# Prompt attention of a decoder step: scores over two pairs of PSUM banks, the last projection tiles by token halves, the conv mixer in pieces, block outputs copied to SBUF

## The reference

```python
gb, gc, u, q, k, v = split(rmsnorm(x) @ w_in)          # 3 x 512 conv mixer, 3 x 512 attention
yconv = gb * causal_dwconv(gc * u, prefix, w3, b)      # width 3, over tokens
s  = einsum('bqhcd,bkhcd->bhcqk', q, k) / 8 + bias     # 4 heads, c = 2 halves of 64; causal, T5 bias
p  = softmax(s)
o  = (p[c=0] - lam * p[c=1]) @ v
yattn = rmsnorm(o) * w * (1 - lam_init)                # per head of 128
x += concat(yconv, yattn) @ w_out
x += cross_attn(rmsnorm(x), memory K/V)
x += conv_ffn(rmsnorm(x))
y  = rmsnorm(x)
```

## Time and profile before

| | |
|---|---|
| time, median of 3 runs | 1035.6 us (1034.36 to 1038.36) |
| the profiled execution | 1035.47 us, span 1033.0 us |
| TensorE busy | 967.5 us (94%) |
| weight loads of TensorE | 884.1 us (86%) |
| VectorE busy | 560.5 us (54%) |
| ScalarE busy | 361.8 us (35%) |
| GpSimd busy | 97.9 us (9%) |
| granted clock of TensorE, mean | 0.98 of full speed |

### The profile page before, as it was taken

One profiled execution on the slowest core, in us unless ns is written; L12 is line 12 of the kernel. 1 busy time (PEld: TensorE's weight loads), 2 busy tenths in 40 slices (PEclk: granted clock), 3 DMA queues, 4 the chain that ended last, 5 costly groups with the idle time before them and its releaser, 6 DMA issues.

```text
span 1033.0 us, 19196 instructions
## 1 busy us (share of the span) xinstructions
PE 967.5 (94%) x7675; PEld 884.1 (86%) x7675; DVE 560.5 (54%) x1021; ACT 361.8 (35%) x670; POOL 97.9 (9%) x213
## 2 busy tenths in 40 slices
PE   5999999978988999999889999999999999999996
PEld 4977766747878999988656999999999999999995
DVE  4544523626677645335433448777347783477643
ACT  4422212223445436234323334343124331234332
POOL 2220000000000012000000002221012220122000
PEclk8999998998999999999999999999999999999998
DMA  8656678841111246624652422233233232323213
GB/s 236 206 175 212 202 240 284 276 158 42 42 41 42 84 123 196 214 81 155 233 205 101 97 82 83 82 98 88 82 91 94 82 88 85 94 85 95 72 37 103
DMA packets 162491, 131.36 MB, mean 127 GB/s; under 512 B 5819, under 2 KB 139222, under 8 KB 162370
## 3 DMA queue, kind: packets, MB, share of 16 engines
q1 hardware_dynamic: 159940, 124.40, 39.0%
q0 software_dynamic: 2320, 5.68, 1.9%
q10 hardware_dynamic: 144, 0.07, 0.0%
HBM read 123.12 MB, written 7.00 MB: 126 GB/s over the span
## 4 chain that ended last, share of the span: by engine, by line
PE 81%; DVE 7%; issue 4%; ACT 3%; SPq 2%; DMA 2%; DVEq 0%; ACTq 0%
PE proj L942 66%; PE T L954 7%; PE score L1031 2%; PE score L1147 1%; PE score L1132 1%; PE score L1059 1%; SPq L665 1%; DVE score L1790 1%; ACT pages L1392 1%; DMA w_raw<-in_w_in 1%; SPq L682 1%; PE score L1165 1%; ACT w_hi L1227 1%; DVE a_lo L1593 1%; DVE norm_area L1587 0%
## 5 line engine op out<-in xcount | busy, mean ns | idle before, releaser
L942 PE MATMUL proj<-a_hi,w_hi 128*128 128x272 f32 (+1 forms) x992 | 222.7, 296 | 4.2 <-DVE a_lo L1593 2.6
L942 PE MATMUL proj<-a_hi,w_lo 128*128 128x272 f32 (+1 forms) x992 | 216.5, 289 | 0.0
L942 PE MATMUL proj<-a_lo,w_hi 128*128 128x272 f32 (+1 forms) x992 | 216.4, 289 | 0.0
L1527 DVE TENSOR_TENSOR w_lo<-w_raw,w_hi 128x1024 fp32r<-128x1024 f32 (+1 forms) x132 | 159.0, 1205 | 62.5 <-ACT w_hi L1227 62.2
L1227 ACT ACTIVATE w_hi<-w_raw 128x1024 fp32r<-128x1024 f32 (+1 forms) x132 | 137.2, 1039 | 159.3 <-PE proj L942 143.0
L942 PEld LDWEIGHTS proj<-a_hi,w_hi 128*128 128x128 f32 x992 | 162.0, 191 | 15.2 <-issue 12.5
L942 PEld LDWEIGHTS proj<-a_lo,w_hi 128*128 128x128 f32 x992 | 162.4, 191 | 0.1
L942 PEld LDWEIGHTS proj<-a_hi,w_lo 128*128 128x128 f32 x992 | 160.9, 191 | 0.0
L942 PE MATMUL proj<-d_hi,w_hi 128*128 128x272 f32 x704 | 145.4, 288 | 0.0
L942 PE MATMUL proj<-d_hi,w_lo 128*128 128x272 f32 x704 | 144.8, 288 | 0.0
L942 PE MATMUL proj<-d_lo,w_hi 128*128 128x272 f32 x704 | 144.6, 287 | 0.0
(11 more groups left out here) (257 smaller groups left out, 1219.3 us busy)
## 6 DMA issues: line engine op xcount, KB each, us to landing
w_raw<-in_w_up SPq DMA_DIRECT2D x44, 512.0 KB, 3.8
w_raw<-in_w_in SPq DMA_DIRECT2D x24, 512.0 KB, 5.0
pages<-in_cache_k SPq DMA_DIRECT2D x40, 256.0 KB, 4.4
early_pages<-in_cache_v SPq DMA_DIRECT2D x40, 256.0 KB, 4.5
w_raw<-in_w_ckv SPq DMA_DIRECT2D x16, 512.0 KB, 3.9
c_pages<-in_cache_mem_k SPq DMA_DIRECT2D x16, 512.0 KB, 6.6
c_pages<-in_cache_mem_v SPq DMA_DIRECT2D x16, 512.0 KB, 5.2
w_raw<-in_w_down SPq DMA_DIRECT2D x16, 448.0 KB, 3.7
```

Of the source, the lines that this page charges most:

```text
L942: mm = pe.matmul(proj[n % 2][:, half, 0:width], wt, act[:, k, half * HALF:half * HALF + width], start=(k == 0 and a == 0), stop=(k == w["k ...
L1527: dve.tensor_tensor(w_lo[:, n % W_RING, 0:kt, :], w_raw[:, n % W_RING, 0:kt, :], w_hi[:, n % W_HI_RING, 0:kt, :].bitcast(F32), ALU.subtrac ...
```

## The change

- The tiles of a channel come as gc, u, gb instead of gb, gc, u.
- The tile before the ticks is gone. The last 8 tiles of w_in (channel 1's u to channel 3's gb) are cut by token halves: half 0 has 24 matmuls over all k for tokens 0 to 271, half 1 the same for the others. Tick u, 0 to 15, has one of them. Both go to `proj[0]`, one bank each, and VectorE empties each bank by itself. A half waits until the same bank's last half is emptied.
- `proj[1]` is free for a second pair of score banks, S2 and S3. Odd units use it. A score waits for the exponentials of two units before.
- ScalarE copies a block's outputs from T1 to `o_blk` and frees T1; the squares are taken from `o_blk`, and `p_scale` works in place there.
- The conv mixer of a channel is four steps (rstd and states; first tap; two taps; gating) placed one by one in ticks 3 to 16, with its own buffer `mixed`.

```diff
-        for j, kind in enumerate(("gb", "gc", "u")):
+        for j, kind in ((1, "gc"), (2, "u"), (0, "gb")):
...
+FIRST_BY_HALF, AFTER_IN = TILE["in", "u", 1], TILE["out", "add", 0]
+BY_HALF = range(FIRST_BY_HALF, AFTER_IN)
...
-        if f[1] == "u":
-            part = part + [("conv", f[2]), ("mix", f[2])]
+        if f == ("in", "gb", 0):
+            part = part + [("conv", 0, part) for part in range(3)] + [("mix", 0)]
...
+    beside = {3: [("conv", 1, 0)], 4: [("conv", 1, 1)], 5: [("conv", 1, 2)], 7: [("mix", 1)],
+              9: [("conv", 2, 0)], 10: [("conv", 2, 1)], 11: [("conv", 2, 2)], 13: [("mix", 2)],
+              14: [("conv", 3, 0)], 15: [("conv", 3, 1), ("conv", 3, 2)], 16: [("mix", 3)]}
+    for u in range(len(units) + 2):
+        if 0 <= u - 1 < len(units):
+            s.append(("p_mix", *units[u - 1]))
+        if u >= 4 and units[u - 4][1] == HEADS - 1:
+            s.append(("p_out", units[u - 4][0]))
+        if u < len(units):
+            s.append(("p_score", *units[u]))
+        if 3 <= u < len(units) + 3 and units[u - 3][1] == HEADS - 1:
+            s.append(("p_scale", units[u - 3][0]))
+        if u == 0:
+            s.append(("s_out", 1))
+        n, half = divmod(u, 2)
+        if n < len(BY_HALF):
+            if half == 0:
+                s.append(("split", FIRST_BY_HALF + n + 2))
+            s += beside.get(u, [])
+            s.append(("half", FIRST_BY_HALF + n, half))
+            if half:
+                s.append(("tile", FIRST_BY_HALF + n))
+        else:
+            s += beside.get(u, [])
+        if 0 <= u - 1 < len(units):
+            s.append(("p_turn", *units[u - 1]))
+        if u == len(units) + 1:
+            s.append(("mem_in",))
+        if 0 <= u - 2 < len(units):
+            s.append(("p_pv", *units[u - 2]))
+            if units[u - 2][1] == HEADS - 1:
+                s += [("p_norm", units[u - 2][0]), ("p_eps", units[u - 2][0])]
+    s += [("p_scale", 3), ("half_tile", AFTER_IN), ("p_out", 3)]
+    s += [("squares", k, "mem") for k in range(KT)]
...
+        if kind == "p_score":
+            uses = [use(slot) for slot in (("S0", "S1"), ("S2", "S3"))[(step[1] * HEADS + step[2]) % 2]]
...
+            def tile_half(n, half):
+                if half == 0:
+                    pe.wait_ge(w_lo_ready, n + 1)
+                    if n == FIRST_BY_HALF:
+                        wait_tile_out(pe, n - 2)
+                if n > FIRST_BY_HALF:
+                    pe.wait_ge(half_out, 2 * (n - 1 - FIRST_BY_HALF) + half + 1)
+                cols = slice(half * HALF, (half + 1) * HALF)
+                out = proj[0][:, half, 0:HALF]
+                for k in range(KT):
+                    w_h, w_l = w_hi[:, n % W_HI_RING, k, :], w_lo[:, n % W_RING, k, :]
+                    pe.matmul(out, w_h, a_hi[:, k, cols], start=(k == 0), stop=False)
+                    pe.matmul(out, w_h, a_lo[:, k, cols], start=False, stop=False)
+                    mm = pe.matmul(out, w_l, a_hi[:, k, cols], start=False, stop=(k == KT - 1))
+                mm.then_inc(tile_done if half else half_done, 1)
...
                 elif kind == "p_out":
-                    wait_taken(pe, *use_of["p_norm", arg][0])
+                    pe.wait_ge(sem("p_scaled"), arg + 1)
...
                 elif kind == "p_norm":
                     wait_full(act, uses[0])
+                    if arg:
+                        act.wait_ge(full["T0"], use_of["p_out", arg - 1][0][1] + 1)
+                    act.activation(o_blk, bank["T1"], ACT.Copy).then_inc(free["T1"], 1)
+                    wait_taken(act, *uses[0])
                     for h in range(HEADS):
                         cols = slice(h * P, (h + 1) * P)
-                        ins = act.activation(o_sq[:, cols], bank["T1"][:, cols], ACT.Square,
+                        ins = act.activation(o_sq[:, cols], o_blk[:, cols], ACT.Square,
...
+                elif kind == "half":
+                    w, half = TILES[arg], step[2]
+                    dve.wait_ge(tile_done if half else half_done, arg + 1 if half else arg - FIRST_BY_HALF + 1)
+                    cols = slice(half * HALF, (half + 1) * HALF)
+                    out = proj[0][:, half, 0:HALF]
+                    if w["kind"] == "u":
...
+                        side(dve.tensor_tensor(pre[:, 2 + half * HALF_P:2 + (half + 1) * HALF_P], out[:, mine],
+                                               gate[:, mine], ALU.mult))
+                        dve.tensor_tensor(pre_s[:, GB * half:GB * half + GB, 2:6],
...
+                    else:
+                        dst = gates[:, int(w["kind"] == "gb"), cols]
+                        if w["kind"] == "gb":
+                            dve.wait_ge(sem("mixer_ready"), w["i"])
+                        dve.tensor_tensor(dst, out, rstd[:, cols], ALU.mult).then_inc(half_out, 1)
...
                 elif kind == "p_scale":
                     dve.wait_ge(sem("p_rstd"), arg + 1)
-                    wait_full(dve, uses[0])
-                    dve.tensor_tensor(o_blk.rearrange("p (h d) -> p h d", h=HEADS), quads["T1"],
-                                      free_dims(small[:, 32:36], 0, [(1, HEADS), (0, DV)]), ALU.mult
-                                      ).then_inc(free["T1"], 1)
+                    o = o_blk.rearrange("p (h d) -> p h d", h=HEADS)
+                    dve.tensor_tensor(o, o, free_dims(small[:, 32:36], 0, [(1, HEADS), (0, DV)]), ALU.mult
+                                      ).then_inc(sem("p_scaled"), 1)
```

More of the change, by code:

```diff
@@ L155, in make_schedule @@
     fill = [("in", "k", h) for h in range(HEADS)] + [("in", "v", h) for h in range(HEADS)]
-    fill += [("in", kind, c) for c in range(CT) for kind in ("gb", "gc", "u")]
+    fill += [("in", kind, c) for c in range(CT) for kind in ("gc", "u", "gb")]
     after = {("in", "k", h): [("k_out", h)] for h in range(HEADS)}
@@ L186, in make_schedule @@
     units = [(i, h) for i in range(SEQ // P) for h in range(HEADS)]
[L188 to L211, removed]
+    assert len(plan) == FIRST_BY_HALF - TILE["in", "k", 0]
     late = []
@@ L919, in tile @@
                 pe.wait_ge(w_lo_ready, n + 1)
-                if n >= 2:
+                if n == AFTER_IN:
+                    wait_tile_out(pe, n - 1)
+                elif n == AFTER_IN + 1:
+                    for slot in ("S2", "S3"):
+                        wait_taken(pe, slot, latest[slot])
+                elif n >= 2:
                     wait_tile_out(pe, n - 2)
@@ L994, in _ @@
                               start=True, stop=True).then_inc(full["S0"], 1)
+                elif kind == "half":
+                    tile_half(*step[1:])
                 elif kind in ("tile", "half_tile"):
-                    tile(arg, latest, kind == "half_tile")
+                    if arg not in BY_HALF:
+                        tile(arg, latest, kind == "half_tile")
                 elif kind in ("k_out", "v_out"):
@@ L1077, in _ @@
                             wait_tile_out(pe, TILE["in", "k", hh])
+                    if (i, h) == (0, 1):
+                        wait_tile_out(pe, FIRST_BY_HALF - 1)
                     for half in range(i // 2 + 1):
@@ L1683, in _ @@
                 elif kind == "conv":
+                    c, part = step[1:]
                     settle()
-                    wait_tile_out(dve, TILE["in", "u", arg])
-                    side(dve.tensor_tensor(by_half(pre[:, 2:2 + SEQ]), by_half(pre[:, 2:2 + SEQ]), prompt(rstd), ALU.mult))
-                    side(dve.tensor_tensor(seqs(pre_s, 2, 6), seqs(pre_s, 2, 6), samples(rstd), ALU.mult))
-                    settle()
-                    dve.wait_ge(sem("pre_zero"), 1)
-                    wait_taken(dve, *use_of["setup_2",][1])
@@ L1696, in _ @@
-                    y = gates[:, 1, :]
-                    done(conv3((pre, pre_s), (prompt(y), samples(y)), cols))
-                elif kind == "mix":
-                    y = gates[:, 1, :]
-                    done(dve.tensor_tensor(y, y, gates[:, 0, :], ALU.mult))
-                    done(dve.tensor_copy(b_hi[:, arg, :], y))
-                    dve.tensor_tensor(b_lo[:, arg, :], y, b_hi[:, arg, :].bitcast(F32), ALU.subtract
+                    cols = [vec[:, j:j + 1] for j in (V_CW + c, V_CW + CT + c, V_CW + 2 * CT + c, V_CB + c)]
@@ L1887, in _ @@
                     out = conv[:, j, :]
-                    ins = conv3((up_pad[:, j, i % 2, :], up_pad_s[:, j, i % 2, :, :]), (prompt(out), samples(out)), cols,
-                                first_tap=False)
+                    ins = conv3((up_pad[:, j, i % 2, :], up_pad_s[:, j, i % 2, :, :]), (prompt(out), samples(out)), cols)
                     ins.then_inc(sem("conv_ffn_done"), 1)
```

109 lines of the change are left out of this document (58 added, 51 removed), and 1 row of the table FILLS.

## The result

| | before | after |
|---|---|---|
| time, median of 20 runs | 1035.5 us (1031.1 to 1039.8) | 1039.8 us (1032.6 to 1042.3) |
| ratio of the runs | | 1.0034, 95% interval 1.0020 to 1.0048 |
| profiled execution: time, span | 1035.47, 1033.0 us | 1035.42, 1033.5 us |
| its mean granted clock | 0.980 | 0.978 |

A forecast was written before the change was run, and what follows sets the result against it. VectorE's queue was taken to set the pace in the prompt attention's blocks, with TensorE busy 94% overall. Terms +2.6 - 3.5 - 2.1 + 2.9 - 2.1 + 3.3 = +1.1 on 1035.5 gave 1036.6, rounded to 1037 us; range 1026 to 1043.

The forecast's parts named there:

- 1. mix of unit 3: Start, ticks 0 to 3: losing the whole tile opens a hole and delays this mix to 240.8, +2.6 us.
- wait before the first score: Start: TensorE waits some 3.8 us for bank S1, which the samples' norm still holds.
- 3. block 1, 2, 3: Ticks 4 to 15: VectorE's queue sets the pace; blocks of 22.3, 24.3, 27.7 us, changes of -3.5, -2.1, +2.9.
- waits for squares: Ticks 5, 9 and 13: VectorE ends waiting for the squares of the block's outputs, 0.9, 1.9 and 1.4 us.
- 4. last hole: After tick 15: no half tile is left, so TensorE waits some 4.4 us for the last mix.
- tail: Chain from the last mix to the last low part: 11.5 us against 13.64 before, -2.1.
- 5. slow stretches, on the path: Behind the holes at start and end: half clock speed, 1.65 us each, +3.3 at most, taken whole.
- VectorE keeps up: Rival for the blocks: VectorE has slack, TensorE never waits after 224.9; 1021 us; chance 0.20 wholly or in part.
- step 5: TensorE's clock: half speed behind the start and end holes, 1.65 us each, +3.3 in all.
- the clock falls in every block: Rival: waits after ticks 6, 10 and 14 bring half speed; six stretches give 1043 us; chance 0.15.
- The waits of the transposes for the mix: Sign in ticks 6 to 15: transposes wait 1 to 2 us each for VectorE's mix, replacing scores' waits for exponentials.
- Step 4: The end: tail 2.1 us shorter; the copy costs 0.6 only here and took away a 3.01 us wait for T1.

The follow-up runs named there:

- e1_warm: Changed kernel plus unread matmuls filling TensorE's four waits (first prompt score, three turns of block outputs): 1033.7 us, ratio 0.9975 to the kernel before.
- c2_split: Changed kernel with the splitting of the next weights moved ahead of the scores: 1035.2 us, ratio 0.9985 to the kernel before.
- c4_both: Changed kernel with the weight splitting ahead of the scores and the first half tile ahead of the first scores: 1034.0 us, ratio 0.9971 to the kernel before.
- e2_mid: c4_both with the step of the block outputs moved from ahead of the scores to right behind them: 1029.8 us, ratio 0.9952 to the kernel before.
- e3_nocopy: Changed kernel without ScalarE's copy of the block outputs; squares and scaling read T1: 1033.3 us, ratio 0.9972 to the kernel before.
- d2_out: Changed kernel with the turn of block outputs moved behind the half tile in ticks 7, 11 and 15: 1046.8 us, ratio 1.0099 to the kernel before.
- g_final: e2_mid without ScalarE's copy, plus unread matmuls ahead of each turn of outputs and the last turn of mixed weights: 1030.0 us, ratio 0.9948 to the kernel before.

## Why the prediction was right, step by step

| step | predicted | measured |
|---|---|---|
| 1. mix of unit 3, against 238.18 | 240.8, +2.6 | 241.78, +3.6 |
| the same from the samples' last product, slow stretch included | +4.25 | +4.20 |
| wait before the first score | 3.8 | 3.41 |
| 3. block 1, 2, 3 | 22.3, 24.3, 27.7 | 22.25, 24.41, 28.24 |
| waits for squares | 0.9, 1.9, 1.4 | 0.93, 1.94, 1.51 |
| turn of block outputs, wait for T0 | none in the sum | 2.47, 2.65, 2.98 |
| 4. last hole | 4.4 | 2.00 |
| tail | 11.5 | 11.80 |
| 5. slow stretches, on the path | 2, at +1.65 each, 3.3 | 4; one at 1.5, three at about 0.5, 2.9 |
| sum, profiled execution | 1036.6 | 1035.4 |

- **VectorE's queue as the bound of the blocks: right in size, too simple in kind.** The three sums held within 0.54 us, and at full clock (e1_warm) the blocks were only 0.4 to 0.6 us shorter. But c2_split took 9.8 us of waits out of this queue and the blocks together became 0.3 shorter, so other loops are nearly as long. The rival "VectorE keeps up" (1021) needed slack that was not there. Where it had truth was in the order: VectorE's waits are waits for ScalarE, and moving steps (c2_split, c4_both, e2_mid) won 0.4 to 0.7% against after.
- **The start: right.** The 2.6 held no slow stretch. That was set apart in step 5, whose own +1.65 came true at 224.3. Together they are 4.25, and from the samples' last product to the mix of unit 3 the traces have 22.39 us against 18.19, +4.20. That product began 0.6 us earlier in after, and so the times on the trace's own scale differ by 3.6 only.
- **The end: the hole was oversized, the sum nearly right.** The hole was 2.0 us and not 4.4. Of the difference 1.5 goes with the slow stretches in the blocks, that of block 3 above all, which the sum did not have: they made TensorE late for its last half, and at full clock (e1_warm) the hole was 3.52. The other 0.9 is the sum's own error. No slow stretch followed the 2.0, so this half of the +3.3 of step 5 did not come. Three others came in the blocks, and the four together cost 2.9 us of the stage (e1_warm), near the 3.3 by luck and not by the places that were named.
- **What was missed: the wait for T0 in each block.** I had taken T0 as free after TensorE's turn, and gave ScalarE's queue only the copy, the squares and the exponentials. Its order (exponentials, w_hi, copy out of T0) makes TensorE wait 2.5 to 3.0 us three times, and the clock falls each time. That is the mechanism of the rival "the clock falls in every block". It was real, at fewer places, and in the trace it cost a third of the price I gave it, since VectorE's queue covered most (e1_warm); what it costs in a median run is open, as said below. The waits of the transposes for the mix that were to show the forecast right, 1 to 2 us each, did not come: before the last hole there was one, 0.36 us. At its full price of 1.65 three stretches would have added 5 us.
- **The copy: mis-sized.** Step 4 had it cost its 0.6 in the tail only and take away a wait of 3.01 us. Without it (e3_nocopy) the blocks were 0.8 to 1.3 us shorter, and TensorE's waits for T1 were 0.97, 1.10 and 0.93 us, inside a wait that it had anyway.
- **The medians.** The step that puts the profiled execution's time equal to a median run failed for after: 1035.4 in the profile, 1039.8 in the median. Each run's span and mean clock give a product, span x (1 - clock), the time lost to the lower clock, idle time at a low clock included. Over 116 runs of before and 33 of after it is 23.3 us (standard error 0.3) and 25.3 (0.5); span x clock is 1010.8 (0.2) and 1011.8 (0.2). Of the 3 us between the means, 1 is in the schedule and 2 go with a lower clock. The traces of both executions of after show 22.3 and 17.7 us lost, the lucky end. The product is an account and not a price: in e1_warm it is 9.4 us lower than in after and the mean span only some 5. Where the 2 us sit in a median run no trace shows, since the stage lost the same 6.8 us to the clock in the first trace of before and in both of after; that filling the four waits brought the runs' loss to 15.9 us says the change's holes have a part in it.

**What the parts were worth.** Blocks 1 and 2 became 3.6 and 2.0 us shorter, and this was given back in block 3 (conv inside) and at the start (the lost whole tile). Some of the 3.6 is the clock, which took 3.4 us of TensorE's work in block 1 of before and 1.7 in that of after. No run took out the token halves, the conv pieces or the new order of tiles by themselves, so their shares aren't shown. The copy cost 5.6 us in the medians, 0.9 in the traced stage. The second pair of banks gained at most 0.3%. Some pieces were badly placed: e2_mid, which keeps all the parts and moves three steps, is 0.5% faster than before, and 0.7% faster than after.

## What to carry to other kernels

When a step is moved, look at every bank it shares and at who frees it in each engine's own order. Both surprises here, the waits of 2.5 to 3.0 us and the 6.6 us of d2_out, were T0 held by one step while another wanted it. A copy that frees a bank early pays only if somebody waits for that bank; ask first what stands behind the copy. A wait on an engine that is not the bound is still worth a look, since cutting it into pieces or filling it can keep the clock up: e1_warm did only the filling and was 0.5% faster than after.

## What the runs showed of the hardware

**Half speed came in stretches of some 3.4 us, 1.7 us of work each, or in multiples of them.** Summing 1 - clock over fine windows gives 6.8, 5.1, 8.5, 10.4, 13.7 or 0 us for the stage, always near a multiple of 1.7. Behind a wait of 2.47 us in after there was one, behind one of 2.14 in e2_mid too, and the 2.00 us wait of after's last hole had none. The Trainium skill, "TensorE: Matmul & The Clock Gate", section "HAM oscillation — how this bites in real kernels", warns of just this drop in each round; the prediction let one stretch without it speak against that, and was wrong there. A wait of the same length doesn't always do it. In c2_split three waits of 3.01, 3.00 and 3.05 us for T0, one in each block, were followed by no half speed, by 6.9 us and by 6.9 us of it. The last hole of 3.52 us in e1_warm had none, that of 3.50 in e3_nocopy did, and its tail was 13.40 instead of 11.8.

**It also comes where TensorE never waits.** In g_final, with TensorE busy all the time and the same work that ran at full speed in e2_mid:

```profile
590.00:591.00 1.00, 1.00 (x10) 0.96 (x10) 0.20 (x1) 1.00 (x2) 0.00 (x0) 0.58 0.71 201
591.00:592.00 1.00, 1.00 (x6) 1.00 (x6) 1.00 (x2) 0.82 (x2) 0.55 (x1) 0.50 0.03 9
...
593.00:594.00 1.00, 1.00 (x8) 1.00 (x8) 0.00 (x0) 0.00 (x0) 0.00 (x0) 0.72 0.00 0
```

What sets these off isn't shown. They go with the spread between runs: over the 33 runs of after, time and mean granted clock have a correlation of -0.91. The work behind the stage, the same in all kernels, took 702.5 to 707.9 us in 14 profiled executions, and less its lost clock 695.5 to 697.6. So where a change is worth under half a per cent, two profiles say nothing of it as wholes. Compare the stage, and leave the verdict to the runs.
